# Hybrid decoder trunk: shared expert's up tiles rounded and subtracted behind the normalized chunks, and another order of eviction and subtraction in the second layer's mixer norm

## The chip, the cores and the metric

One Trainium2 chip, one core of it. The metric is the device time of one execution in microseconds (us), less is better. The program is a single launch that reads all inputs from HBM and writes the final output. The names used for the engines are TensorE (PE in the rows, PEld for its weight loads), VectorE (DVE), ScalarE (ACT), GpSimd (POOL) and SyncE (SP), whose queue issues most DMAs.

## What is computed

Two layers over a sequence of 256 tokens with 1024 features, all in float32. Each layer is a token mixer and a mixture of experts (MoE); before each stands an RMSNorm with a scale and a shift per feature. The first layer's mixer is differential attention, the second's is retention.

```python
for i in range(DEPTH):                       # DEPTH = 2
    mod = jax.nn.silu(c) @ ada_w[i] + ada_b[i]
    sh_a, sc_a, g_a, sh_f, sc_f, g_f = jnp.split(mod[:, None, :], 6, axis=-1)
    h = rmsnorm(x, norm_mix[i]) * (1.0 + sc_a) + sh_a
    y = diff_attention(h, ...) if i == 0 else retention(h, ...)
    x = x + g_a * y
    h = rmsnorm(x, norm_ffn[i]) * (1.0 + sc_f) + sh_f
    x = x + g_f * moe(h, ...)
return rmsnorm(x, final_norm)

def moe(xm, router_w, router_b, w1, w3, w2, s_w1, s_w3, s_w2):
    scores = jax.nn.sigmoid((xt @ router_w).astype(jnp.float32))
    choice = scores + router_b        # the best 4 of 8 groups, then the best 8 of 64 experts
    ...
    shared = (jax.nn.silu(xt @ s_w1) * (xt @ s_w3)) @ s_w2
    return (acc[:T] + shared).reshape(B, S, D)
```

The routed experts' part, `acc`, gathers each expert's tokens, runs its two up products and its down product, and adds the weighted result. The shared expert runs over all tokens; its up weights `s_w1` and `s_w3` are 1024x256 each, and the change is about them.

## The kernel before

**Products in three parts.** The products of the mixers, the router and the shared expert's up layer are done with both operands split in two: a rounded high part and the rest. `product` (line 936) issues three matmuls for each: high times high, high times low, low times high. So a weight tile of 128x2048 is handled twice before TensorE may use it: ScalarE rounds it (`round_w`, line 634, the cast on line 637, semaphore `w_hi`), and VectorE subtracts the rounded copy from the tile and leaves the low part in its place (`low_part`, lines 1407 to 1410, semaphore `w_lo`). The tiles have one fixed order, `split` (line 315), which is the order in which both semaphores count.

**The norm.** There are four norms ahead of the last one; their number n is 0 for the first layer's mixer, 1 for its MoE, 2 for the second layer's mixer, 3 for its MoE. For each of the two blocks of 128 tokens ScalarE squares and takes a root (`norm_stats`, line 587), VectorE takes the reciprocal and scales (`norm_root`, lines 1397 and 1402), TensorE turns the block with eight 128x128 transposes (`turn_h`, line 920). The turned input is eight chunks of 128 features in four PSUM banks, two chunks (a pair, m = 0 to 3) in a bank. Then in `evict_hT` ScalarE evicts pairs 0 and 2 with scale and shift (line 612), VectorE pairs 1 and 3 (line 1419), each two instructions of 128x256. ScalarE rounds each pair (line 622, `hT_rounded`; it waits for pairs 1 and 3 on VectorE's `hT_dve`), and VectorE's `low(m)` subtracts (line 1426, `hT_split`). TensorE's next products take the pairs in order and wait in `hT_there` (line 932) for each pair's `low`.

**The MoE's head.** After norm 1 or 3 TensorE computes the router's logits, 24 matmuls (line 938 by way of `product`, from line 1003). ScalarE takes the sigmoid (line 687), TensorE turns the scores back (line 1011), and VectorE does the routing in a long chain of small instructions that begins with the copy on line 1471 and has the chosen experts ready at line 1501. TensorE meanwhile computes the first half of the shared up product, tile 0, 48 matmuls; it waits for that tile's `w_lo`. Then it waits for the chosen experts (`chosen_ready`), ranks them with a few small matmuls (lines 1018 to 1025), does half of tile 1's product (24 matmuls), places the experts (lines 1031 and 1032), and does the other half. VectorE then writes the table of experts and passes (line 1538, `route_ready`). ScalarE's Silu of the up product (line 691) gives two ring slots free (`release(2)`), for which SP has DMAs of expert weights waiting; further expert loads wait for `route_ready`. After the shared down product (line 1045) the loop over experts begins.

**Order.** All orders around the change are written out by hand: each engine's queue is in program order, and semaphores join them. On ScalarE `moe(l)` (line 671) issued the rounding of tile 0 ahead of `norm_stats`, the rounding of tile 1 right behind it, then the table load for Sigmoid with a dummy instruction (line 677), then `evict_hT`. On VectorE `moe(l)` (line 1452) issued `norm_root`, tile 0's `low_part`, `evict_hT`, tile 1's `low_part`; in the first layer a small addition (`later_rows(9)`, line 1620) follows, and then the routing. In norms with n > 0 VectorE's `evict_hT` issued `evict(1)`, `low(0)` only after it, `evict(3)`, then `low(1)` to `low(3)`. `part_high` (line 683) makes bf16 copies for the routed experts and isn't needed until line 1460.

Of the kernel before, what the change touches and what calls it, by code (L numbers as in the profile page):

```python
# [59 lines left out]
def trunk(nc, x, c, norm_mix, norm_ffn, ada_w, ada_b, da_w_in, da_w_out, da_lq1, da_lk1, da_lq2, da_lk2,  # L60
# [18 lines left out]
    with ExitStack() as ctx:  # L79
# [492 lines left out]
        def _(act):  # L572
# [61 lines left out]
            def round_w(*key):  # L634
                if key in split:
                    arrived(act, where[key])
                    nc.scalar.copy(high_of(key), slot(where[key])).then_inc(w_hi, 1)
# [33 lines left out]
            def moe(l):  # L671
# [1 line left out]
                    load_root_table()  # L673
                round_w("shared", l, 0)
                norm_stats()
                round_w("shared", l, 1)
                nc.scalar.activation(lexp[:, 0:1], ident[:, 0:1], ACT.Sigmoid)
                if l == 0:
                    release_ada(9)
                evict_hT()  # L680

                def part_high(tc):
                    nc.scalar.copy(parts[:, tc, 0, :], h[:, tc, :]).then_inc(part_hi, 1)

                part_high(0)
                act.wait_ge(logits_done, l + 1)
                nc.scalar.activation(scoreT, banks[0][:, 0:T], ACT.Sigmoid).then_inc(scoresT_ready, 1)
                part_high(1)
                nc.scalar.activation(lexp[:, 0:1], ident[:, 0:1], ACT.Silu)
                act.wait_ge(sh_up, l + 1)  # L690
# [81 lines left out]
            for part in range(3):  # L772
                n, i = 4 * part, 3 * part + 2
# [605 lines left out]
        def _(dve):  # L1379
# [32 lines left out]
            def evict_hT():  # L1412
                n = norms[0] - 1

                def evict(m):
                    dve.wait_ge(h_turned, 4 * n + m + 1)
                    for kk in range(2):
                        k = 2 * m + kk
                        ins = nc.vector.tensor_scalar(hT_full[:, k, :], banks[m][:, T * kk:T * kk + T],
                                                      mod_T[:, n // 2, 3 * (n % 2) + 1, k:k + 1],  # L1420
                                                      mod_T[:, n // 2, 3 * (n % 2), k:k + 1], ALU.mult, ALU.add)
                    ins.then_inc(hT_dve, 1)
# [4 lines left out]
                                            hT_hi[:, 2 * m:2 * m + 2, :], ALU.subtract).then_inc(hT_split, 1)  # L1427

                dve.wait_ge(mod_T_in[n], 1 if n == 0 else 16)
                evict(1)  # L1430
                if n == 0:
                    low_part("mix_in", 0, 0)
                low(0)
                if n > 0:
                    evict(3)
                for m in range(1, 4):
# [14 lines left out]

            def moe(l):
                norm_root()
                low_part("shared", l, 0)
                evict_hT()
                low_part("shared", l, 1)

                def rest_part(tc):
# [380 lines left out]
```

## Time and profile before

| | us |
|---|---|
| median of 3 runs | 1429.36 (1429.16 to 1429.58) |
| time of the profiled execution | 1428.65 |
| its span in the profile | 1426.9 |
| TensorE matmul busy | 1328.6 (93% of the span) |
| VectorE busy | 550.8 (39%) |
| ScalarE busy | 448.5 (31%) |
| HBM read | 514.10 MB, 361 GB/s over the span |

Stages of the profiled execution, from the page's 40 slices and the timeline: the first layer's mixer up to 198 us, its MoE head from 198 to 236, its loop over experts to 698, the second layer's mixer with its norm to 913.5, its MoE head to about 950, its experts and the last norm to the end. In the expert loops the DMA engines are busy all the time (422 GB/s in the slices); in the second mixer they have room (119 GB/s in the lowest slice), and TensorE is busy in all slices.

How to read it: the share of an engine over the whole span says little, since the stages have different limits. In a head or a norm the engines hand work to one another, and what counts is which of two queues comes last to a meeting point. A time in a timeline row is where the first instruction of the row starts, the next number how long the row takes; a number in brackets is the idle time before it with what ended that idle time.

### The profile page before, as it was taken

The page shows a single profiled execution, that of the slowest core. Times are in us where ns is not written, and L with a number is a line of the kernel's source. Part 1 is how long each engine was busy: PE and PEld are TensorE (multiplying, and loading weights), DVE is VectorE, ACT ScalarE, POOL GpSimd, SP SyncE. Part 2 cuts the span into 40 slices and gives each one's busy share as a digit, 9 for nine tenths or more (in the row PEclk, how much of TensorE's full clock was granted, in tenths as well). Part 3 has the DMA queues.
Part 4 walks back from the last instruction along what each step waited for, and adds up shares of the span by engine and source line. Part 5 has one row for each costly group of instructions (what it writes and reads, how often), then busy time and mean ns, then how long its engine had stood idle before and what let it go on. Part 6 is the DMA issues. An engine that isn't in the chain of part 4 may idle for free.

```text
span 1426.9 us, 32982 instructions
## 1 busy us (share of the span) xinstructions
PE 1328.6 (93%) x12029; PEld 875.0 (61%) x12030; DVE 550.8 (39%) x1227; ACT 448.5 (31%) x890; POOL 207.6 (15%) x663
## 2 busy tenths in 40 slices
PE   4999889999999999989799999799999999999996
PEld 2877666555556555544599998665555555555553
DVE  2556565332323322222534455653332323322334
ACT  3443451222222222221444454522222222222222
POOL 8200102111111111111000000011111111111110
PEclk8999999999999999999899999899999999999999
DMA  9999995999999999999995434449999999999995
GB/s 351 352 385 398 407 383 224 421 421 422 422 422 422 422 422 422 422 422 421 376 298 188 159 119 148 162 181 421 420 422 422 422 421 422 422 422 422 422 422 216
DMA packets 113338, 516.06 MB, mean 362 GB/s; under 512 B 9632, under 2 KB 46624, under 8 KB 63360
## 3 DMA queue, kind: packets, MB, share of 16 engines
q1 hardware_dynamic: 109920, 509.64, 89.1%
q0 software_dynamic: 2656, 3.49, 0.9%
q10 hardware_dynamic: 704, 2.10, 0.4%
q8 instruction: 44, 0.72, 0.2%
q14 instruction: 14, 0.11, 0.0%
HBM read 514.10 MB, written 1.09 MB: 361 GB/s over the span
## 4 chain that ended last, share of the span: by engine, by line
PE 68%; DMA 11%; SPq 6%; DVE 5%; ACT 5%; issue 3%; POOL 1%; ACTq 1%; DVEq 0%; POOLq 0%
PE bank L938 18%; PE bank L1120 15%; PE bank L1141 7%; PE bank L1123 7%; PE bank L1055 6%; DMA ring<-in_exp_w_dram 6%; PE bank L1096 5%; PE bank L1147 3%; SPq L347 3%; DMA ring<-in_da_w_in_dram 2%; DMA mods<-in_exp_w_dram 2%; SPq L350 2%; PE bank L913 2%; DVE arena L1579 1%; PE bank L1130 1%
## 5 line engine op out<-in xcount | busy, mean ns | idle before, releaser
L1120 PE MATMUL bank<-ring,arena 128*64 128x512 f32 x768 | 178.6, 605 | 9.9 <-DMA ring<-in_exp_w_dram 9.9
L1096 PEld LDWEIGHTS bank<-arena 128*128 128x128 bf16 x3264 | 142.1, 98 | 55.5 <-issue 55.0
L1055 PE MATMUL bank<-arena_r 128*128 128x512 f32 x560 | 161.2, 418 | 3.0 <-DVE arena_r L1591 3.0
L1591 DVE TENSOR_TENSOR arena_r<-bank,arena_r 128x512 fp32r<-128x512 f32 x136 | 94.0, 692 | 154.2 <-ACT arena_r L726 154.2
L1096 PE MATMUL bank<-arena 128*128 128x64 bf16 (+1 forms) x3264 | 151.8, 207 | 0.0
L719 ACT ACTIVATE arena<-bank 128x256 f32<-128x256 f32 (+1 forms) x68 | 22.6, 333 | 387.4 <-PE bank L1120 270.1
L726 ACT CAST arena_r<-bank 128x512 fp32r<-128x512 f32 x136 | 79.7, 586 | 189.4 <-PE bank L1141 124.8
L543 POOL TENSOR_TENSOR arena<-arena,pass_base 128x2 f32 x136 | 23.6, 197 | 743.2 <-PE bank L1107 729.2
L1055 PEld LDWEIGHTS bank<-arena_r 128*128 128x128 f32 x560 | 94.6, 188 | 60.2 <-issue 47.5
L938 PE MATMUL bank<-HH_r,ring_r 128*128 128x256 f32 x448 | 128.4, 287 | 0.0
L1120 PEld LDWEIGHTS bank<-ring,arena 128*64 128x64 f32 x768 | 56.5, 139 | 111.4 <-issue 110.8
L1565 DVE TENSOR_SCALAR arena<-bank,mod_T 128x128 f32<-128x128 f32 x272 | 92.9, 404 | 72.0 <-PE bank L1096 72.0
L714 ACT ACTIVATE arena<-bank,mod_T 128x128 f32<-128x128 f32 x272 | 102.5, 457 | 53.2 <-PE bank L1096 53.2
L1579 DVE SCALAR_TENSOR_TENSOR arena<-bank,arena 128x256 f32<-128x256 f32 x35 | 23.5, 671 | 236.8 <-ACT arena L719 236.8
L1123 PE MATMUL bank<-ring,arena 128*32 128x256 f32 x1472 | 91.5, 390 | 7.8 <-ACT arena L714 7.8
L938 PE MATMUL bank<-HH_r,mods_r 128*128 128x256 f32 x288 | 84.5, 293 | 6.2 <-DVE mods_r L1426 6.2
L938 PEld LDWEIGHTS bank<-HH_r,ring_r 128*128 128x128 f32 x448 | 88.0, 196 | 0.0
L1141 PE MATMUL bank<-ring,arena 128*64 128x512 f32 x384 | 87.7, 598 | 0.0
L1123 PEld LDWEIGHTS bank<-ring,arena 128*32 128x32 f32 x1472 | 76.0, 108 | 13.8 <-issue 8.8
L938 PE MATMUL bank<-mods_r 128*128 128x256 f32 x288 | 83.3, 289 | 0.0
L1120 PE MATMUL bank<-mods,arena 128*64 128x512 f32 x176 | 77.8, 595 | 3.8 <-DMA mods<-in_exp_w_dram 3.8
L938 PE MATMUL bank<-HH_r 128*128 128x256 f32 x272 | 78.6, 289 | 0.3 <-DVE ring_r L1409 0.3
(273 smaller groups left out, 2158.3 us busy)
## 6 DMA issues: line engine op xcount, KB each, us to landing
ring<-in_exp_w_dram SPq DMA_DIRECT2D x264, 1024.0 KB, 24.0
ring<-in_ada_w_dram SPq DMA_DIRECT2D x48, 1024.0 KB, 13.6
HH<-in_exp_w_dram SPq DMA_DIRECT2D x40, 1024.0 KB, 21.0
mods<-in_exp_w_dram SPq DMA_DIRECT2D x40, 1024.0 KB, 25.0
arena<-in_exp_w_dram SPq DMA_DIRECT2D x40, 1024.0 KB, 25.1
ring<-in_ret_w_in_dram SPq DMA_DIRECT2D x24, 1024.0 KB, 11.9
ring<-in_da_w_in_dram SPq DMA_DIRECT2D x12, 1024.0 KB, 17.3
ring<-in_ret_w_out_dram SPq DMA_DIRECT2D x8, 1024.0 KB, 4.9
```

Source lines behind the costliest of these rows:

```text
L347: sp.dma_start(place.rearrange("p (k n) -> p k n", k=KD), w.rearrange("o (p k) n -> p (o k) n", k=KD)).then_inc(done, 16)
L714: ins = nc.scalar.activation(to, got, ACT.Identity, scale=mod_T[:, l, 4, k:k + 1], bias=mod_T[:, l, 3, k:k + 1])
L726: nc.scalar.copy(y[:, 0, 512 * hf:512 * hf + 512], banks[hf][:, :]).then_inc(u["y_hi"], 1)
L938: ins = nc.tensor.matmul(out, a[x1], b[x2], start=(first and i == 0), stop=(last and i == 2), skip_group_check=True)
L1055: ins = nc.tensor.matmul(banks[4 + NH * tc + hf][:, :], S[:, P * tc:P * tc + P], y[:, r, 512 * hf:512 * hf + 512], start=False, stop=(last ...
L1096: ins = nc.tensor.matmul(banks[2 - 2 * half][:, P * kk:P * kk + 2 * W], parts[:, tc, r, P * (4 * half + kk):P * (4 * half + kk + 1)], Pg[: ...
L1120: ins = nc.tensor.matmul(banks[1][W * i:W * i + W, :], xg[:, k, W * i:W * i + W], w13[j][:, k, :, :], start=(k == 0), stop=(k == KD - 1))
L1123: ins = nc.tensor.matmul(banks[1][W * i:W * i + W, 0:256], xg[:, k, W * i:W * i + W], w13[j].rearrange("p k w (n b) -> p k b w n", b=2)[:, ...
L1141: ins = nc.tensor.matmul(banks[hf][W * j:W * j + W, :], ehT[:, b, W * j:W * j + W], w2[j][:, b, 512 * hf:512 * hf + 512], start=(b == 0), ...
L1147: ins = nc.tensor.matmul(banks[hf][W * i:W * i + W, :], ehT[:, 0, W * i:W * i + W], w2[j][:, b, 512 * hf:512 * hf + 512], start=True, stop ...
L1565: ins = nc.vector.tensor_scalar(to, got, mod_T[:, l, 4, k:k + 1], mod_T[:, l, 3, k:k + 1], ALU.mult, ALU.add)
L1591: nc.vector.tensor_tensor(y[:, 1, 512 * hf:512 * hf + 512], banks[hf][:, :], y[:, 0, 512 * hf:512 * hf + 512], ALU.subtract).then_inc(u[f" ...
```

## The change

Three edits, in two functions on ScalarE and VectorE:

1. ScalarE, both MoE heads: the rounding of the shared expert's second up tile moves behind `evict_hT`, and `part_high(0)` behind the sigmoid of the logits.
2. VectorE, both MoE heads: the subtraction of the shared expert's first up tile moves behind `evict_hT`, so that both tiles' subtractions stand there, one behind the other.
3. VectorE, norm 2 only (the second layer's mixer): `low(0)` is issued ahead of `evict(1)`.

No instruction is added or removed, and no semaphore's count changes. TensorE's, GpSimd's and SP's instructions are the same as before.

```diff
@@ ScalarE, moe(l)
                 round_w("shared", l, 0)
                 norm_stats()
-                round_w("shared", l, 1)
                 nc.scalar.activation(lexp[:, 0:1], ident[:, 0:1], ACT.Sigmoid)
                 if l == 0:
                     release_ada(9)
                 evict_hT()
+                round_w("shared", l, 1)
 
                 def part_high(tc):
                     nc.scalar.copy(parts[:, tc, 0, :], h[:, tc, :]).then_inc(part_hi, 1)
 
-                part_high(0)
                 act.wait_ge(logits_done, l + 1)
                 nc.scalar.activation(scoreT, banks[0][:, 0:T], ACT.Sigmoid).then_inc(scoresT_ready, 1)
+                part_high(0)
                 part_high(1)
@@ VectorE, evict_hT()
                 dve.wait_ge(mod_T_in[n], 1 if n == 0 else 16)
-                evict(1)
+                if n != 2:
+                    evict(1)
                 if n == 0:
                     low_part("mix_in", 0, 0)
                 low(0)
+                if n == 2:
+                    evict(1)
                 if n > 0:
                     evict(3)
                 for m in range(1, 4):
@@ VectorE, moe(l)
                 norm_root()
+                evict_hT()
                 low_part("shared", l, 0)
-                evict_hT()
                 low_part("shared", l, 1)
```

**The change on VectorE in the first layer's MoE head**, from the reciprocal of the second token block to the start of the routing. `ring2` is the ring slot with the shared expert's first two tiles, `arena_r` their rounded copies, `mods`, `HH_r` and `mods_r` the normalized chunks, their high and their low part. Before:

```order
L1397 RECIPROCAL rs<-rs 128x1 [waits root]
L1402 TENSOR_SCALAR HH<-X,rs 128x1024 [waits dve_step]
L1409 TENSOR_TENSOR ring2_r<-ring2,arena_r 128x2048 [waits w_hi]
L1419 TENSOR_SCALAR mods<-bank1,mod_T 128x256 [waits h_turned,mod_T_in1]
L1419 TENSOR_SCALAR mods<-bank1,mod_T 128x256
L1426 TENSOR_TENSOR mods_r<-mods,HH_r 128x512 [waits hT_rounded]
L1419 TENSOR_SCALAR mods<-bank3,mod_T 128x256 [waits h_turned]
L1419 TENSOR_SCALAR mods<-bank3,mod_T 128x256
L1426 TENSOR_TENSOR mods_r<-mods,HH_r 128x512 [waits hT_rounded] x3
L1409 TENSOR_TENSOR ring2_r<-ring2,arena_r 128x2048 [waits w_hi]
L1620 TENSOR_TENSOR mods<-bank4,mods 128x256 [waits ada_done]
L1471 COPY arena<-bank2 128x128 [waits bank_rows_read,late_consts_in,scores_ready]
```

Now:

```order
L1397 RECIPROCAL rs<-rs 128x1 [waits root]
L1402 TENSOR_SCALAR HH<-X,rs 128x1024 [waits dve_step]
L1419 TENSOR_SCALAR mods<-bank1,mod_T 128x256 [waits h_turned,mod_T_in1]
L1419 TENSOR_SCALAR mods<-bank1,mod_T 128x256
L1426 TENSOR_TENSOR mods_r<-mods,HH_r 128x512 [waits hT_rounded]
L1419 TENSOR_SCALAR mods<-bank3,mod_T 128x256 [waits h_turned]
L1419 TENSOR_SCALAR mods<-bank3,mod_T 128x256
L1426 TENSOR_TENSOR mods_r<-mods,HH_r 128x512 [waits hT_rounded] x3
L1409 TENSOR_TENSOR ring2_r<-ring2,arena_r 128x2048 [waits w_hi] x2
L1623 TENSOR_TENSOR mods<-bank4,mods 128x256 [waits ada_done]
L1474 COPY arena<-bank2 128x128 [waits bank_rows_read,late_consts_in,scores_ready]
```

The first 128x2048 subtraction has moved from ahead of the chunks to behind them; both now stand between the last chunk's `low` and the routing. Lines from 1430 on are three higher in the changed kernel.

**The change on ScalarE in the same place**, from the last root of the norm to the sigmoid of the logits. Before:

```order
L601 ACTIVATE rs<-ss,eps 128x1 [waits sumsq]
L637 CAST arena_r<-ring2 128x2048 [waits landed5]
L677 ACT_TABLE_LOAD
L677 ACTIVATE lexp<-ident 128x1
L612 ACTIVATE mods<-bank0,mod_T 128x256 [waits ada_done,h_turned,mod_T_in1]
...
L622 CAST HH_r<-mods 128x512 [waits hT_dve]
L683 CAST arena<-HH 128x1024
L687 ACTIVATE arena<-bank0 128x256 [waits logits_done]
L683 CAST arena<-HH 128x1024
```

Now:

```order
L601 ACTIVATE rs<-ss,eps 128x1 [waits sumsq]
L676 ACT_TABLE_LOAD
L676 ACTIVATE lexp<-ident 128x1
L612 ACTIVATE mods<-bank0,mod_T 128x256 [waits ada_done,h_turned,mod_T_in1]
...
L622 CAST HH_r<-mods 128x512 [waits hT_dve]
L637 CAST arena_r<-ring2 128x2048 [waits landed5]
L686 ACTIVATE arena<-bank0 128x256 [waits logits_done]
L683 CAST arena<-HH 128x1024 x2
```

The cast of the 128x2048 tile has moved from ahead of the table load to behind the last chunk's cast, and the first bf16 copy behind the sigmoid.

## Rows read from the trace of the kernel before

**Rows 1.** The profile's page, the chain that ended last, share by engine.

```profile
PE 68%; DMA 11%; SPq 6%; DVE 5%; ACT 5%; issue 3%; POOL 1%; ACTq 1%; DVEq 0%; POOLq 0%
```

**Rows 2.** Timeline of VectorE, first MoE head: start, us, line, shapes, [idle before <- releaser].

```profile
204.43 2.28 DVE L1409 TENSOR_TENSOR ring_r<-ring,arena_r 128x2048 fp32r<-128x2048 f32 x1
...
208.01 0.69 DVE L1426 TENSOR_TENSOR mods_r<-mods,HH_r 128x512 fp32r<-128x512 f32 x1 [0.39 <-ACT HH_r L622]
...
211.33 2.28 DVE L1409 TENSOR_TENSOR ring_r<-ring,arena_r 128x2048 fp32r<-128x2048 f32 x1
213.53 0.42 DVE L1620 TENSOR_TENSOR mods<-bank,mods 128x256 f32<-128x256 f32 x1
214.54 0.29 DVE L1471 COPY arena<-bank 128x128 f32<-128x128 f32 x1 [0.59 <-PE bank L1011]
```

**Rows 3.** Timeline of ScalarE, the same place.

```profile
203.01 1.90 ACT L637 CAST arena_r<-ring 128x2048 fp32r<-128x2048 f32 x1
...
206.32 1.00 ACT L612 ACTIVATE mods<-bank,mod_T 128x256 f32<-128x256 f32 x2
207.36 0.62 ACT L622 CAST HH_r<-mods 128x512 fp32r<-128x512 f32 x1
...
213.62 0.38 ACT L687 ACTIVATE arena<-bank 128x256 f32<-128x256 f32 x1 [2.23 <-PE bank L938]
```

**Rows 4.** Timeline of TensorE, the same place.

```profile
204.57 1.09 PE L925 MATMUL bank<-ident,HH 128*128 128x128 f32 x8 [0.31 <-DVE HH L1402]
208.85 0.46 PE L938 MATMUL bank<-HH_r,arena_r 128*128 128x256 f32 x1 [3.19 <-DVE mods_r L1426]
...
220.36 0.19 PE L1018 MATMUL bank<-arena,upper 128*128 128x64 bf16 x1
```

**Rows 5.** Timeline of VectorE, second MoE head.

```profile
920.96 2.28 DVE L1409 TENSOR_TENSOR ring_r<-ring,arena_r 128x2048 fp32r<-128x2048 f32 x1
...
924.52 0.69 DVE L1426 TENSOR_TENSOR mods_r<-mods,HH_r 128x512 fp32r<-128x512 f32 x1 [0.38 <-ACT HH_r L622]
...
931.18 0.29 DVE L1471 COPY arena<-bank 128x128 f32<-128x128 f32 x1 [1.06 <-PE bank L1011]
```

**Rows 6.** Timeline of TensorE, second MoE head.

```profile
919.69 3.68 PE L925 MATMUL bank<-ident,HH 128*128 128x128 f32 x16 [6.20 <-DVE HH L1402]
925.36 0.55 PE L938 MATMUL bank<-HH_r,arena_r 128*128 128x256 f32 x1 [1.99 <-DVE mods_r L1426]
```

**Rows 7.** Timeline of VectorE, norm 2, the second layer's mixer.

```profile
708.30 0.99 DVE L1419 TENSOR_SCALAR mods<-bank,mod_T 128x256 f32<-128x256 f32 x2
709.21 0.68 DVE L1426 TENSOR_TENSOR mods_r<-mods,HH_r 128x512 fp32r<-128x512 f32 x1
...
710.71 1.88 DVE L1426 TENSOR_TENSOR mods_r<-mods,HH_r 128x512 fp32r<-128x512 f32 x3
```

**Rows 8.** Timeline of ScalarE, norm 2.

```profile
708.14 0.62 ACT L622 CAST HH_r<-mods 128x512 fp32r<-128x512 f32 x1
```

**Rows 9.** Timeline of TensorE, norm 2: the first product's first matmuls.

```profile
710.03 0.55 PE L938 MATMUL bank<-HH_r,mods_r 128*128 128x256 f32 x1 [1.76 <-DVE mods_r L1426]
...
711.45 0.57 PE L938 MATMUL bank<-HH_r,mods_r 128*128 128x256 f32 x1
```

**Rows 10.** Windows: stretch, length, busy us of PE, PEld, DVE, ACT, POOL, PEclk, DMA share, GB/s.

```profile
172.50:178.20 5.70, 5.70 (x14) 4.44 (x15) 2.89 (x7) 3.47 (x6) 2.75 (x4) 0.50 1.03 407
208.85:212.36 3.51, 3.51 (x16) 3.33 (x17) 3.51 (x6) 2.54 (x5) 0.00 (x0) 0.51 1.02 429
212.36:213.60 1.24, 1.23 (x10) 1.02 (x9) 1.24 (x2) 0.00 (x0) 0.00 (x0) 1.00 1.00 423
371.30:377.40 6.10, 3.42 (x17) 1.44 (x18) 0.53 (x3) 0.00 (x0) 1.58 (x4) 1.00 1.01 419
550.40:557.00 6.60, 3.96 (x13) 1.58 (x14) 0.49 (x3) 0.00 (x0) 1.58 (x4) 0.75 1.01 422
710.00:714.10 4.10, 4.07 (x18) 4.01 (x19) 3.42 (x6) 3.12 (x4) 0.00 (x0) 0.50 1.09 349
```

## The prediction

> **What bounds the kernel now.** I read the page first, for the chain that ended last: TensorE holds 68% of it, and VectorE and ScalarE 5% each [rows 1]. Those small shares are the norms and the MoE heads, where the change lies. There the chain goes from queue to queue, so I read the timelines of three engines at three places, and ask at each what comes last.
>
> *First MoE head.* ScalarE casts the second up tile (203.01, 1.90 us) before it may load its table and evict the first pair at 206.32 [rows 3]. VectorE spends 2.28 us on the first tile from 204.43 on [rows 2]. But the eight transposes of the second block are through at 204.57 + 1.09 = 205.66 [rows 4], so both engines are late for the chunks. The first product starts at 208.85 after 3.19 us of standstill [rows 4], the sigmoid follows at 213.62 [rows 3], and the routing at 214.54, where VectorE has idled for 0.59 us [rows 2]. Until then the meeting point is TensorE's and ScalarE's. From 214.54 on it is VectorE's: the ranks' matmul at 220.36 [rows 4] waits for the routing, and the rest of the head for the ranks. So the question is not when the first product starts, but **when VectorE can start the routing**.
>
> *Second MoE head.* The same: first product at 925.36 [rows 6], routing at 931.18 after 1.06 us idle [rows 5].
>
> *Norm 2.* Here TensorE goes from the first product at 710.03 [rows 9] straight into the mixer, so a later stream of products is a later end.
>
> **First MoE head, worked out.** Edits 1 and 2 go together. ScalarE reaches its table load at 203.01 instead of 204.91; load and dummy take what they took from there to 206.32, 1.41 us, so it is free at 204.42. The transposes are spaced (1.09 - 0.28)/7 = 0.12 us, taking 0.28 for one; the second of the block ends at about 205.0, and the first eviction starts there instead of at 206.32. From that start to `low(0)` it took 208.01 - 206.32 = 1.69 us (the cast at 207.36 with 0.62 lies between) [rows 2, 3], so `low(0)` runs at 206.72, 1.29 us earlier, with VectorE's `evict(1)` (from 205.25, some 0.99 long) done in time. The first product moves with it, to 207.56.
>
> Now VectorE's account. From `low(0)` to the end of the last `low` are 211.33 - 208.01 = 3.32 us, so 210.04. Then come **two** tile subtractions instead of one, each 213.53 - 211.33 = 2.20 us: 214.44. `later_rows` takes 0.42, and the routing starts at about 214.90 instead of 214.54 [rows 2]. **Term: +0.36 us.** The work is the same; the idle time has moved from behind it (0.59) and `low(0)` (0.39) to ahead of the evictions, where it can't be used, and there is slightly more of it. TensorE isn't last any more: even with all 24 logits matmuls at the low clock its logits end by about 212.4, 1.2 us before 213.62, and the scores are there 0.92 us later (213.62 to 214.54), at 213.3. `part_high(0)` costs nothing: it moves into ScalarE's wait behind the sigmoid. Tile 0's low part is ready at 212.3 instead of 206.7, and TensorE, behind the scores' transposes, wants it between 212 and 213, so this hardly costs; tile 1's cast on ScalarE now ends at about 211.0, ahead of VectorE's need at 212.24.
>
> **Second MoE head.** The transposes run slower here, 16 in 3.68 us [rows 6], spaced 0.21 us, so the tenth, which ends the first pair, is there at 922.1. `low(0)` is at 922.14 + 1.69 = 923.83, only 0.69 us earlier than 924.52. Then 3.32 and twice 2.20: 931.55, and with nothing between, the routing starts at 931.57 instead of 931.18 [rows 5]. **Term: +0.39 us.**
>
> **Norm 2 (edit 3).** VectorE is free at 708.30 [rows 7]. The cast it needs ends at 708.14 + 0.62 = 708.76 [rows 8], so `low(0)` starts at 708.80 instead of 709.21, and the first product at 709.62 instead of 710.03 [rows 9]. But `low(1)` now has two evictions between: 708.80 + 0.60 + twice 0.91 (708.30 to 709.21) = 711.23 instead of 710.71 [rows 7], **0.52 us later**. ScalarE's cast of pair 1 waits for `evict(1)` (done at 710.4) and ends at 711.06, just in time. TensorE does its first six matmuls from 709.62, stands still from about 711.0, and starts the second pair at 711.45 + 0.52 = 711.97 or a little later [rows 9]. All later products are behind that.
>
> What this costs depends on the clock. TensorE is at 0.50 here until 714.1, so at 1.2 GHz, then at 2.4 [rows 10]. A matmul takes 3.51/16 = 0.22 us at the lower and 1.24/10 = 0.12 at the higher level [rows 10], so a microsecond at the lower loses 0.45 us. If the clock rises at 714.1 as before, the lag of 0.52 shrinks to about 0.52 x 0.12/0.22 = 0.29 us. But the rise came 4.1 us after the products began (710.03 to 714.1), elsewhere 3.5 us (208.85 to 212.36) and 5.7 us (172.50 to 178.20) [rows 10], each after an unbroken run of matmuls. The run is broken now. If it has to begin anew at 712.0, the rise is at 715.5 to 717.7 instead of 714.1: 1.4 to 3.6 us more at the lower level, a loss of 0.6 to 1.6, middle 1.1. I take that, since every row with a rise has an unbroken run before it. **Term: 0.29 + 1.1 = +1.4 us**, bounds +0.2 (rise unchanged, a little of the first product's gain kept) and +1.9.
>
> **Sum.** 0.36 + 1.4 + 0.39 = +2.15 us. None of it is absorbed behind: the expert loads that SP holds back come after Silu and after `route_ready`, so they move along with the head, and TensorE and the DMA queues alternate on the chain from there on. The profiled execution (1428.65 us) would become 1430.8; the median of the runs before is 0.71 us above it, and I forecast against the median: **1431.5 us**, +0.15%. A measurement of this kernel can tell about 0.2%, 2.9 us, from no change.
>
> **Rivals.**
>
> *The clock falls in the new hole: slower.* TensorE did tile 0's 48 matmuls right up to the ranks at 220.36; now it is done with them 1.2 to 1.9 us sooner and waits for a routing that starts 0.36 later. That makes a standstill of about 1.8 to 2.2 us in the first head and 1.0 to 1.5 in the second. The rows show both outcomes of somewhat longer ones: after 2.7 us at 371.30 the clock stayed at 1.00, after 2.6 us at 550.40 it fell (0.75 over the stretch of 6.6, so about 3.3 us at the lower level) [rows 10]. If it falls here, 3.4 us at 1.2 GHz lie on tile 1's 48 matmuls, which release ranks, Silu and the expert loads: 3.4 x 0.45 = 1.5 us each time. It decides from one such fall on top of my sum: 2.15 + 1.5 = 3.65, 1433.0 us; with both 1434.5. For it: a hole only 0.5 us shorter than one that fell. Against: of two such holes only one fell, and these are shorter. Chance 0.22.
> The Trainium skill ("TensorE: Matmul & The Clock Gate", "Why this matters for your kernels") advises to avoid long idle gaps between bursts of matmuls, with a bound longer than any hole named here; by it no fall would come and 1431.5 would stand, yet the hole at 550.40 is under its bound and fell, so the row decides and the rival keeps its chance.
>
> *The clock rises at 714.1 as before in norm 2.* The sum is 0.36 + 0.29 + 0.39 = 1.04: 1430.4 us. For it: the second run is interrupted for only a microsecond. Chance 0.22.
>
> *TensorE, not VectorE, was what the routing waited for, and stays it: faster.* Then the earlier first products count in full: -1.29 and -0.69, with +0.29 in norm 2: -1.7, 1427.7 us. The idle 0.59 and 1.06 us before the routing speak for it; against it that 2.20 us of tile work now stand where only that idle time was. It would need VectorE's two subtractions to cost 1.1 us each. Chance 0.04.
>
> *The shift of the heads is absorbed* in the expert loops, whose DMA runs all the time, and the norm's by nothing: about 1429.4 to 1430.8. Chance 0.07. That the change doesn't do what it says is excluded by the orders shown.
>
> **How the numbers follow.** The forecast case (1431.5, bounds 1430.3 to 1432.3 from norm 2's term and a few tenths on the others) has 0.45. The range takes in the two mild cases below it and the fall with one loss above it: 1429.4 to 1433.5, which leaves out the faster case, the double fall and about half a tenth more at each end. Faster by over 0.2% (under 1426.5) is reached by no case but luck with the clock: 0.03. Slower by over 0.2% (over 1432.2) holds the clock's fall, 0.22, and the top of the forecast case, 0.04: 0.26. Within 0.2%: 0.71.
>
> **What would show it.** In both heads: `low(0)` about 1.3 and 0.7 us earlier against the transposes; VectorE without idle time before line 1474; line 1018 some 0.4 us later; TensorE idle before it for 1 to 2.2 us, with PEclk telling about the rival. In norm 2: a hole of about 1 us behind the first six matmuls, and PEclk at 0.50 beyond 714.5. I am wrong if the routing starts earlier than before against the transposes' end, if the hole behind the six matmuls isn't there, or if the expert loops take a different time.

## The result, and the profile after

The changed kernel took 1432.42 us (median of 8 runs, 1430.72 to 1434.42), the kernel before beside it 1429.08 (8 runs, 1428.36 to 1429.58): a ratio of 1.0024, 95% interval 1.0013 to 1.0035. The change costs 3.3 us by the medians; the interval alone would allow 1.9 to 5.0. Its profiled execution took 1432.12 us, 3.5 more than that of before.

I cut both profiles into stages. Each head is measured from the start of line 1402 on the second token block, the last thing ahead of the transposes on VectorE. "Routing" is the start of the copy with which VectorE's routing chain begins (line 1471, now 1474), "shared down" the first matmul of the shared down product (line 1045), and a hole is a stretch in which TensorE stands still:

| us | before | after | difference |
|---|---|---|---|
| span start to head 1's scaling | 203.33 | 204.44 | +1.11 |
| head 1: scaling to `low(0)` / first product / routing | 4.68 / 5.52 / 11.21 | 3.46 / 4.30 / 11.81 | -1.22 / -1.22 / +0.60 |
| head 1: scaling to first matmul of shared down | 25.32 | 25.92 | +0.60 |
| from there to norm 2's scaling (experts, same code) | 476.37 | 476.28 | -0.09 |
| norm 2: scaling to `low(0)` / first product | 4.19 / 5.01 | 3.84 / 4.68 | -0.35 / -0.33 |
| norm 2 and mixer ("mixer stage" below), to head 2's scaling | 214.84 | 216.41 | +1.57 |
| head 2: scaling to `low(0)` / first product / routing | 4.66 / 5.50 / 11.32 | 4.04 / 4.88 / 11.77 | -0.62 / -0.62 / +0.45 |
| head 2: scaling to first matmul of shared down | 25.44 | 25.87 | +0.43 |
| rest (same code) | 481.63 | 481.47 | -0.16 |

In all three places the first product is earlier, and what counts behind it is later. The +1.11 at the start is in code that the change doesn't touch. There the profiles scatter from 202.4 to 204.6 in all kernels but the two that put work on GpSimd.

VectorE's timeline of the changed kernel, first head (start, us, line, shapes, [idle before <- releaser]), for [rows 2]:

```profile
206.42 0.99 DVE L1419 TENSOR_SCALAR mods<-bank,mod_T 128x256 f32<-128x256 f32 x2 [0.82 <-PE bank L925]
207.90 0.69 DVE L1426 TENSOR_TENSOR mods_r<-mods,HH_r 128x512 fp32r<-128x512 f32 x1 [0.48 <-ACT HH_r L622]
...
211.22 4.49 DVE L1409 TENSOR_TENSOR ring_r<-ring,arena_r 128x2048 fp32r<-128x2048 f32 x2
215.62 0.42 DVE L1623 TENSOR_TENSOR mods<-bank,mods 128x256 f32<-128x256 f32 x1
216.25 0.29 DVE L1474 COPY arena<-bank 128x128 f32<-128x128 f32 x1 [0.21 <-DVE mods L1623]
```

The 0.59 us ahead of the routing are gone, and 0.82 stand ahead of the evictions in their place. What is left ahead of line 1474 is released by VectorE itself. The chain that ended last, same place (start, us, engine, what, line), now runs through VectorE from `low(0)` to the routing; its pieces from `low(1)` to line 1623:

```profile
209.50 1.80 DVE mods_r L1426 x3
211.30 4.40 DVE ring_r L1409 x2
215.71 0.35 DVE mods L1623
```

TensorE's timeline there, for [rows 4], and two windows (stretch, length, busy us of PE, PEld, DVE, ACT, POOL, PEclk, DMA share, GB/s):

```profile
208.74 0.36 PE L938 MATMUL bank<-HH_r,arena_r 128*128 128x256 f32 x1 [1.99 <-DVE mods_r L1426]
...
222.07 0.19 PE L1018 MATMUL bank<-arena,upper 128*128 128x64 bf16 x1 [1.42 <-DVE arena L1504]
```

```profile
220.60:222.10 1.50, 0.09 (x3) 0.07 (x3) 1.22 (x8) 0.00 (x0) 0.10 (x1) 1.00 0.66 251
222.10:225.00 2.90, 2.90 (x28) 2.83 (x29) 2.26 (x15) 0.00 (x0) 0.77 (x2) 1.00 0.16 59
```

The hole ahead of the ranks is there, 1.42 us, and in this execution the clock stayed up behind it. Norm 2, for [rows 7, 9, 10]: VectorE, TensorE, a window.

```profile
710.48 0.69 DVE L1426 TENSOR_TENSOR mods_r<-mods,HH_r 128x512 fp32r<-128x512 f32 x1 [0.48 <-ACT HH_r L622]
711.09 1.90 DVE L1419 TENSOR_SCALAR mods<-bank,mod_T 128x256 f32<-128x256 f32 x4
712.90 1.89 DVE L1426 TENSOR_TENSOR mods_r<-mods,HH_r 128x512 fp32r<-128x512 f32 x3
```

```profile
711.32 0.55 PE L938 MATMUL bank<-HH_r,mods_r 128*128 128x256 f32 x1 [1.43 <-DVE mods_r L1426]
...
713.64 0.58 PE L938 MATMUL bank<-HH_r,mods_r 128*128 128x256 f32 x1 [0.70 <-DVE mods_r L1426]
```

```profile
711.30:718.50 7.20, 6.48 (x29) 6.21 (x29) 5.78 (x8) 3.46 (x5) 0.00 (x0) 0.50 1.09 351
```

The four evictions now stand between `low(0)` and `low(1)`, TensorE stands still for 0.70 us behind its first six matmuls, and the clock stays at 0.50 for 7.2 us after the start of the first product instead of 4.1. The second pair's products start 7.00 us after the scaling instead of 6.43.

### The profile page after: what moved, and what is told of

Same layout as the page of the kernel before. It is cut to its first block, busy times and chain, and to the rows that moved or that the text cites. A ratio compares the mean times of both kernels' runs of the same rounds, so it can differ in the third digit from the quotient of the medians.

```text
span 1430.4 us, 32982 instructions
## 1 busy us (share of the span) xinstructions
PE 1330.2 (93%) x12029; PEld 877.2 (61%) x12030; DVE 550.8 (39%) x1227; ACT 448.8 (31%) x890; POOL 208.0 (15%) x663
## 4 chain that ended last, share of the span: by engine, by line
PE 70%; DMA 11%; DVE 7%; ACT 4%; SPq 4%; issue 3%; ACTq 1%; DVEq 0%
PE bank L938 18%; PE bank L1120 16%; PE bank L1141 8%; PE bank L1123 7%; PE bank L1055 6%; DMA ring<-in_exp_w_dram 6%; PE bank L1096 5%; PE bank L1147 4%; SPq L347 2%; DMA mods<-in_exp_w_dram 2%; PE bank L913 2%; DVE arena L1582 1%; DMA ring<-in_ada_w_dram 1%; DVE ring_r L1409 1%; DMA ring<-in_da_w_in_dram 1%
```

## The experiments

My theory: VectorE's queue sets the routing in the heads (edit 2 costs, edit 1 gives), and the broken stream in norm 2 delays the clock. The rivals: TensorE or the clock sets the routing; the clock falls in the new hole. Edit 1 is ScalarE's reordering, edit 2 VectorE's in `moe`, edit 3 that in norm 2. Every kernel computes all of the reference. A run's own milestones count from the same line 1402 as in the table. Each ratio comes with its 95% interval and is not the quotient of the two medians beside it; where the two differ, the ratio counts.

**Edit 1 alone.**

```
-                round_w("shared", l, 1)
                 nc.scalar.activation(lexp[:, 0:1], ident[:, 0:1], ACT.Sigmoid)
                 evict_hT()
+                round_w("shared", l, 1)
...
-                part_high(0)
                 act.wait_ge(logits_done, l + 1)
                 nc.scalar.activation(scoreT, ...)
+                part_high(0)
```

> ScalarE's edit alone (edit 1), VectorE as before. My theory, that VectorE's queue decides in the changed heads: here only one tile subtraction stands ahead of the routing's copy behind the chunks, so VectorE has room; low(0) starts where VectorE's tile subtraction and its first eviction are done, 0.47 us earlier in the first head and 0.45 in the second, and TensorE stays what the routing waits for: routing 0.4 to 0.5 us earlier in both heads, 0.9 us less in all, about 1428.2 against 1429.1. Rival, that the later rounding of tile 1 on ScalarE is itself what delays the routing or tile 1's product: no gain or up to 0.5 us more per head, 1429 to 1430.

Measured: 1427.96 us (11 runs) beside 1428.73 for before (35 runs); ratio 1.0000 (0.9991 to 1.0008). First products 0.51 and 0.48 us earlier, the routing only 0.11 and 0.24. The gain expected of edit 1 is mostly not there. Where it went, the kernel with edit 1 and fills tells, further down.

**Edit 2 alone.**

```
                 norm_root()
+                evict_hT()
                 low_part("shared", l, 0)
-                evict_hT()
                 low_part("shared", l, 1)
```

> VectorE's head edit alone (edit 2), ScalarE as before. My theory: ScalarE still evicts as late as before, so low(0) doesn't move, and VectorE has two tile subtractions (2 x 2.20 us) behind the chunks: routing at 211.33 + 4.40 + 0.42 + 0.2 for the completion of later_rows = 216.35 against 214.54 in the first head (+1.8), and 927.84 + 4.40 = 932.25 against 931.18 in the second (+1.1): +2.9 us, about 1432. Rival, that TensorE's first product decides: no change, since the first product starts as before, 1429.1.

Measured: 1433.21 us (12 runs), ratio 1.0027 (1.0015 to 1.0039). The routing is 1.82 us later in head 1 and 1.07 in head 2. The first products did not move (5.52 and 5.50 us). Its holes ahead of line 1018 are 1.92 and 0.68 us. Behind the first the clock fell: from routing to shared down 15.58 us instead of 14.11. VectorE and TensorE, first head:

```profile
212.60 4.49 DVE L1409 TENSOR_TENSOR ring_r<-ring,arena_r 128x2048 fp32r<-128x2048 f32 x2
...
217.63 0.29 DVE L1471 COPY arena<-bank 128x128 f32<-128x128 f32 x1 [0.21 <-DVE mods L1620]
...
223.43 0.19 PE L1018 MATMUL bank<-arena,upper 128*128 128x64 bf16 x1 [1.92 <-DVE arena L1501]
```

**Edits 1 and 2**, norm 2 as before.

> Edits 1 and 2 together, norm 2 as before. My theory: the heads of the changed kernel as profiled, routing +0.60 us in the first and +0.4 in the second against the norm's end: +1.0 us, about 1430.1, with the rest of the changed kernel's +3.3 in norm 2. Rival, that the clock's fall in TensorE's new hole ahead of the ranks makes most of the loss: +2.5 to +4 us here, and PEclk under 1.00 over tile 1's product in the profile.

Measured: 1430.38 us (11 runs), ratio 1.0011 (1.0002 to 1.0021). The routing stands at 11.81 and 11.77 us, as in the changed kernel to 0.01. In head 1 the clock fell. TensorE's timeline and windows of this kernel:

```profile
221.19 0.19 PE L1018 MATMUL bank<-arena,upper 128*128 128x64 bf16 x1 [1.55 <-DVE arena L1501]
```

```profile
219.30:221.20 1.90, 0.35 (x4) 0.18 (x4) 1.61 (x9) 0.00 (x0) 0.18 (x2) 1.00 0.51 172
221.20:222.40 1.20, 1.20 (x13) 1.14 (x14) 0.67 (x5) 0.00 (x0) 0.80 (x2) 1.00 0.42 167
222.40:225.80 3.40, 3.40 (x18) 3.40 (x17) 2.08 (x13) 0.00 (x0) 0.00 (x0) 0.50 0.02 6
225.80:229.00 3.20, 3.20 (x28) 3.01 (x27) 2.38 (x7) 0.00 (x0) 0.00 (x0) 1.00 0.00 0
```

After a hole of 1.55 us the granted clock went to 0.50 for 3.4 us, in the middle of tile 1's products. Shared down came at 27.39 instead of 25.92: 1.47 us, where the rival said 1.5. The Trainium skill ("TensorE: Matmul & The Clock Gate", "Why this matters for your kernels") warns of gaps longer than this one; here the row decides, and a shorter gap was enough.

**Edit 3 alone.**

```
-                evict(1)
+                if n != 2:
+                    evict(1)
...
                 low(0)
+                if n == 2:
+                    evict(1)
```

> Edit 3 alone: low(0) ahead of evict(1) in norm 2. My theory: low(1) is 0.5 to 0.6 us later, TensorE stands still for about 0.7 us behind its first six matmuls, and the clock rises later: between +0.3 (rise unmoved) and +1.9 us, middle +1.4 to +1.6, about 1430.6, and with more spread from run to run than before, since the moment of the rise decides. Rival, that norm 2 costs only the 0.5 us of the later pair: +0.3 to +0.5 us and no more spread, 1429.5.

Measured: 1429.83 us (12 runs), ratio 1.0006 (0.9998 to 1.0015). Mixer stage 216.09 us, 1.25 more than before; median 1.1 more, 0.9 by the ratio, with zero just inside the interval.

**Tile 0's subtraction on GpSimd.** The changed kernel, with VectorE doing tile 1 alone.

```
+            def pool_low_part(*key):
+                pool.wait_ge(w_hi, split.index(key) + 1)
+                pool.wait_ge(w_lo, split.index(key))
+                nc.gpsimd.tensor_tensor(slot_r(where[key]), slot(where[key]), high_of(key), ALU.subtract).then_inc(w_lo, 1)
...
                 evict_hT()
-                low_part("shared", l, 0)
+                dve.wait_ge(w_lo, split.index(("shared", l, 1)))
                 low_part("shared", l, 1)
```

> The changed kernel with one of the two tile subtractions taken off VectorE: GpSimd does tile 0 (it stands idle there), VectorE tile 1. My theory, that VectorE's queue decides when the routing starts in the changed heads: one 2.20 us less on it, so the routing starts when the scores are there, 1.0 to 1.3 us sooner in each head than in the changed kernel (10.5 to 10.8 us after the second block's scaling instead of 11.8), TensorE's hole ahead of the ranks shrinks to under 0.5 us, and the whole is 2 to 3 us under the changed kernel, about 1429 to 1429.5 with norm 2 as changed. Rival, that the scores decide: routing within 0.2 us of 11.8, no gain. What could spoil the test: VectorE's instructions longer while GpSimd works.

Measured: 1435.63 us (6 runs) beside 1429.25 for before (21 runs), ratio 1.0039 (1.0025 to 1.0054). The test was spoiled by what it put in. GpSimd's subtraction, and VectorE's scaling beside it and without it:

```profile
199.91 4.85 POOL L520 TENSOR_TENSOR ring_r<-ring,arena_r 128x2048 fp32r<-128x2048 f32 x1 [22.41 <-ACT arena_r L646]
```

```profile
201.42 4.27 DVE L1411 TENSOR_SCALAR HH<-X,rs 128x1024 f32<-128x1024 f32 x1
...
205.80 1.16 DVE L1411 TENSOR_SCALAR HH<-X,rs 128x1024 f32<-128x1024 f32 x1
...
214.29 2.29 DVE L1418 TENSOR_TENSOR ring_r<-ring,arena_r 128x2048 fp32r<-128x2048 f32 x1 [0.94 <-ACT arena_r L646]
```

VectorE's scaling took 4.27 us instead of 1.16, and the stages that hold the two stalls are longer by some 2 us each (205.80 us to head 1's scaling, mixer stage 218.25). Counted from the second block's scaling, which comes behind the stall, the heads can still be read: the routing stood at 11.33 and 11.26 us, 0.5 before the changed kernel's, the holes ahead of the ranks were 0.85 and 0.11 us, and the clock fell behind neither. That is against the rival (within 0.2 of 11.8), and less than the 1.0 to 1.3 us expected: with one subtraction VectorE waited 0.94 us for ScalarE's cast of tile 1.

**TensorE kept busy, in the kernel before and in the changed one.** Matmuls of a constant against itself ahead of and behind the transposes, into a bank that is unused there:

```
+            def fill(count, bank):
+                for _ in range(count):
+                    nc.tensor.matmul(bank[:, 0:P], ident[:, :], ident[:, :], start=True, stop=True)
             def turn_h():
+                fill({2: 36, 3: 44}.get(norms[0], 0), banks[3])
...
+                fill({1: 14, 2: 20, 3: 14}.get(norms[0], 0), banks[5])
```

> The kernel before with idle stretches of TensorE filled: matmuls of identity by identity into a bank that nobody reads then, 36 and 44 ahead of the transposes of norms 2 and 3, and 14, 20, 14 behind those of norms 1, 2, 3. It computes the same. My theory, that the lower clock is what makes norm 2 and part of the heads long: PEclk 1.00 through norm 2, 16 transposes of norm 3 in about 2.2 us instead of 3.68, the mixer stage shorter by 1.5 to 2.2 us, the heads' routing 0.5 to 1.5 us earlier, 3 to 4.5 us less in all, about 1425, and less spread between runs. Rival, that the filling only delays the transposes or leaves the clock as it is: the same or slower, 1428.7 to 1431.

> The changed kernel with the same filling. My theory: with the clock held up, edit 3 costs nothing any more (ScalarE's cast of pair 0 is there when VectorE is free, low(1) within 0.1 us of the filled kernel before, and TensorE catches up at 2.4 GHz): mixer stage within 0.3 us of the filled kernel before, instead of +1.6 us unfilled. The heads still wait for VectorE's two tile subtractions, and worse against the filled kernel before, where the routing is no longer held by low-clock products: +1 to +2 us over both heads. Rival, that edit 3's cost is the later pair itself and not the clock: +0.5 us or more in the mixer stage here too.

Measured: 1431.27 us (12 runs), ratio 1.0010 (1.0001 to 1.0020), and 1434.10 (10 runs), ratio 1.0032 (1.0023 to 1.0041). The fills were too long. TensorE in norm 2, with the fill of before:

```profile
697.91 8.20 PE L922 MATMUL bank<-ident 128*128 128x128 f32 x72
```

36 matmuls show as 72 passes of 0.11 us. In norm 2 the first product came 8.07 us after the scaling instead of 5.0, in head 2 at 8.1 instead of 5.5. Only head 1 can be read. In the kernel before, the first product is unmoved at 5.52 and the routing at 10.83 instead of 11.21. The higher clock on the logits brings 0.38 us, and then VectorE's own queue is the limit, with nothing but the 0.21 us of waiting for its own last subtraction ahead of the routing. In the changed kernel the fill put off the first product from 4.30 to 5.20, and the routing stayed at 11.82: TensorE's start doesn't set it there.

**Both subtractions on GpSimd**, edit 1, norm 2 as before.

> Edit 1 (ScalarE), norm 2 as before, and both tile subtractions of each head on GpSimd, none on VectorE. My theory: routing when the scores are there, 0.5 to 1 us earlier than in the kernel before in both heads, 1 to 2 us less in all, about 1427.5; TensorE's tile 0 product then waits for GpSimd only if its subtraction takes over 8 us. Rival: GpSimd's subtraction is so slow (over 4 us) that tile 1 comes after the ranks and TensorE waits for it, or it slows VectorE beside it: no gain or slower.

Measured: 1437.22 us (6 runs), ratio 1.0056 (1.0037 to 1.0076). Low parts come so late that shared down stands at 28.18 and 29.19 us, and in norm 2's stage and at the start VectorE is held again. It can't tell where the routing would be, but the clock fell behind both of its holes ahead of the ranks, 1.56 and 2.91 us.

**Fills of the right length** (20 and 22 ahead of norm 2's and head 2's transposes, 10, 11 and 10 behind those of head 1, norm 2, head 2): in the kernel before, with edit 1 alone, and in the changed kernel. They are called held, since with the fills the granted clock is 1.00 from the transposes to the routing in both heads, and all through the mixer stage.

> The kernel before with a filling cut to size: each fp32 matmul of identity by identity shows as two passes of 0.11 us, so 20 and 22 ahead of the transposes of norms 2 and 3, and 10, 11, 10 behind those of norms 1, 2, 3. My theory: nothing is delayed (first products 5.5, 5.0, 5.5 us after the second block's scaling, as in the kernel before), PEclk 1.00 through both heads and norm 2; the first head's routing is then VectorE's account alone, 4.68 + 3.32 + 2.20 + 0.63 = 10.83 us, the second head's 4.66 + 3.32 + 2.24 = 10.2 instead of 11.3, and the mixer stage 1.3 us shorter than 214.84: 2.8 us less in all, about 1426.3. Rival, that the clock's level in these places isn't worth it, because the chain lies on VectorE and ScalarE there: 0 to 1 us less.

> Edit 1 alone with the same filling. My theory: edit 1's earlier chunks weren't worth more because TensorE ran the logits at the lower clock; with the clock held, the routing follows VectorE's account: 4.18 + 3.32 + 2.20 + 0.63 = 10.3 us in the first head, 9.7 to 9.8 in the second: 0.4 to 0.5 us per head under the held kernel before, about 1425.3, under both kernels. Rival: the later cast of tile 1 on ScalarE delays VectorE's second subtraction (VectorE idle ahead of it), no gain over the held kernel before.

> The changed kernel with the same filling. My theory: edit 3's cost is the clock's, so the mixer stage is within 0.3 us of the held kernel before; the heads' routing stays on VectorE's account with two subtractions behind the chunks: 11.8 us in the first head (1.0 over the held kernel before) and 11.1 in the second (+0.9), and TensorE's hole ahead of the ranks is longer, 2 us and more, so that the clock may fall there for another 1.5 us: 2 to 4 us over the held kernel before, 1428.2 to 1430. Rival, that edit 3 costs by the later pair itself: mixer stage +0.5 us or more.

Measured, beside 1428.74 for before (29 runs):

| | us | ratio (interval) | first product, heads | routing, heads | mixer stage |
|---|---|---|---|---|---|
| before, held | 1426.24 (12 runs) | 0.9979 (0.9971 to 0.9988) | 5.52, 5.52 | 10.84, 10.29 | 213.69 |
| edit 1, held | 1427.07 (11) | 0.9984 (0.9975 to 0.9993) | 5.02, 5.02 | 11.11, 10.49 | 213.69 |
| changed, held | 1430.85 (12) | 1.0011 (1.0002 to 1.0021) | 4.30, 4.30 | 11.82, 11.19 | 213.95 |

Here the clock on the logits can't be the reason any more. First products 0.50 and 1.22 us earlier go with routings 0.2 to 0.3 and 0.9 to 1.0 us **later**. For edit 1, VectorE's timeline of that kernel tells why:

```profile
208.18 1.89 DVE L1432 TENSOR_TENSOR mods_r<-mods,HH_r 128x512 fp32r<-128x512 f32 x3
...
210.75 2.29 DVE L1415 TENSOR_TENSOR ring_r<-ring,arena_r 128x2048 fp32r<-128x2048 f32 x1 [0.69 <-ACT arena_r L637]
```

VectorE waits 0.69 us for ScalarE's cast of tile 1, which edit 1 has put behind the chunks. So edit 1's gain at the front is given back at the next meeting of the two engines. TensorE in the held changed kernel, first head and norm 2:

```profile
220.64 0.19 PE L1024 MATMUL bank<-arena,upper 128*128 128x64 bf16 x1 [2.48 <-DVE arena L1510]
```

```profile
713.05 0.38 PE L944 MATMUL bank<-HH_r,mods_r 128*128 128x256 f32 x1 [1.21 <-DVE mods_r L1432]
```

In norm 2 the changed kernel's hole grew to 1.21 us (0.47 in the held kernel before), and still it cost only 213.95 - 213.69 = 0.26 us. That is how much later the second pair's products start (6.68 us after the scaling instead of 6.42): with the clock at the higher level from the start, nothing of edit 3 but this lag is left. Behind the holes of the heads, 2.48 and 1.83 us, the clock fell both times (routing to shared down 15.60 and 15.58 us).

**The hole ahead of the ranks filled**, and nothing else, in the changed kernel:

```
                     if i == 1:
+                        fill(4, banks[5])
                         pe.wait_ge(chosen_ready, l + 1)
```

> The changed kernel with only its new hole filled: four matmuls of identity by identity (0.9 us) ahead of TensorE's wait for the chosen experts in both heads, everything else as changed, norm 2 unfilled. It computes the same. My theory, that the hole lets the clock fall in about half of the heads (5 of 10 in the profiles of kernels with edit 2, none of 12 without it) at 1.48 us each: no fall in either head here, 14.1 us from the routing's copy to the down product in both, the routing itself where it was (11.8 us), and the median 1 to 2 us under the changed kernel, about 1430 to 1431 where the kernel before has 1428.7. Rival, that the fall isn't the hole's doing or isn't on the path: median as the changed kernel's (+3.3), or a fall seen in a head in spite of the filling.

Measured: 1431.16 us (11 runs) beside 1428.26 for before (15 runs), ratio 1.0014 (1.0005 to 1.0023). TensorE's timeline, first head:

```profile
219.16 1.05 PE L922 MATMUL bank<-ident 128*128 128x128 f32 x8
...
220.66 0.20 PE L1023 MATMUL bank<-arena,upper 128*128 128x64 bf16 x1 [0.44 <-DVE arena L1509]
```

The routing stays at 11.82 and 11.77 us, the hole shrinks to 0.44, and the clock fell in neither head (14.03 and 14.02 us from routing to shared down). The point estimate drops from 1.0024 to 1.0014, about 1.4 us, but the intervals overlap, they come from different experiments, and over the kernel before beside each the medians differ by only 0.4 us (+3.3 and +2.9). In the profile the cure did what was expected, though the changed kernel's own profile had no fall either; the times only point the same way.

## Why the prediction was right, and where it wasn't

**The number.** Forecast 1431.5 us, range 1429.4 to 1433.5; measured 1432.42, inside the range. As a difference it is less good: +2.15 us forecast, +3.3 measured. The direction and the two places of the loss were forecast for the reasons that the runs show; a third component, the falling clock, stood only as a rival, and the range holds the result with its help.

**The bound in the heads: right.** "When can VectorE start the routing" was the right question, and with both subtractions behind the chunks VectorE's own queue is the answer. Edit 2 alone made the routing later by 1.82 and 1.07 us with no change on ScalarE; the first products of the changed kernel were 1.22 and 0.62 us earlier (predicted 1.29 and 0.69) and the routing still later. The rival by which TensorE goes on setting the routing is dead: in the filled kernel the first product was put off by 0.9 us, and the routing didn't move. (The sum by which that rival needed subtractions of 1.1 us was off: 213.25 - 0.42 - 210.04, halved, is 1.4. With 2.20 measured it changes nothing.) Another reading was wrong too. The logits were to end by 212.4 even with all 24 matmuls at the low clock; 207.56 + 24 x 0.22 is 212.8, and measured from the scaling they ended 9.53 us behind it instead of 10.26, only 0.7 us sooner, not 1.2. That costs the routing nothing, but it makes the hole shorter: tile 0's products ended 0.72 and 0.44 us sooner, not 1.2 to 1.9, and the holes were 1.42 and 0.96 us where 1.8 to 2.2 and 1.0 to 1.5 were forecast.

**Head 1's term, +0.36: undersized.** It measured +0.60. The sum left out the 0.21 us for which VectorE stands idle until the completion of its own line 1623 (after, `[0.21 <-DVE mods L1623]`). Before, that wait was hidden in the 0.59 us of waiting for the scores [rows 2]. I counted the removed idle time, not a second wait under it. **Head 2's term, +0.39,** measured +0.45 at the routing and +0.43 at shared down.

**Norm 2's term, 0.29 + 1.1.** The lag was right in kind: the second pair's products started 0.57 us later, forecast 0.52. That the stage cost 0.26 with the clock held is close to 0.29 by luck, for there the lag itself was 0.26 and not 0.52. For the clock, 7.2 us to the rise instead of 4.1 is inside the 1.4 to 3.6 us more that I named, and the stage measured +1.57 against +1.4. How much of it belongs to the change is less sure. In the four profiles whose norm 2 is that of before, without fills and without work on GpSimd, the clock was up for good 4.1 to 6.0 us after the first product's start, and the stage scattered from 214.84 to 215.71; in edit 3's three profiles without fills in norm 2 it was so after 6.5, 7.2 and 7.2 us, and the stage took 216.09, 216.41 and 216.41, more than in any of the four. Edit 3 alone gives 0.9 us by the ratio. So 0.9 to 1.6 us, most of it clock; seven profiles can't say more.

**The step that fell short: a forecast case without a fall.** I gave the fall of the clock in the new hole a chance of 0.22 as an alternative. It comes in about half of the heads instead, and belongs into the sum as a share. Profiles with edit 2 and no fill in the hole show ten heads. The clock stayed up behind holes of 0.68, 0.72, 0.96, 1.42 and once 1.83 us, and fell behind 1.55, 1.83, 1.92 and twice 2.48 us. It also fell in the two heads with both subtractions on GpSimd, behind 1.56 and 2.91. In 12 heads with VectorE's old order (before, edit 1, edit 3 and the fills in them) it never fell, and their longest hole was 1.40 us. So it is the length of the hole that goes with the fall; the order of the work only makes the hole. Each fall costs 1.48 us; the rival's 3.4 x 0.45 = 1.5 was right to a few hundredths. The changed kernel's own profile happened to have none. Its runs spread over 3.7 us, those of before beside them over 1.2 (in the other experiments before spread by up to 6.6, so the spread alone proves nothing).

The account: 1.03 in the heads, 0.9 to 1.6 in norm 2, together 1.9 to 2.6; measured 3.3, with an interval (1.9 to 5.0) that would bear the sum without any fall. The rest, 0.7 to 1.4 us, would be 0.5 to 0.9 falls in an execution. Other kernels point the same way. Edits 1 and 2 cost 1.6 us by the ratio, 1.03 of it at the routing; edit 2 alone 3.9, 2.9 of it at the routing: 0.4 and 0.7 falls are left. In the held pair the mean granted clock over all executions was 0.9887 before (12 runs) and 0.9868 changed (12 runs). A fall of 3.4 us lowers the mean of an execution by 0.5 x 3.4/1429 = 0.0012, so the difference would be, as an estimate, 1.6 falls, give or take 0.8; the mean times differ by 4.4 us, and 2.1 of lag leave 1.5 falls. For the profiled execution the sum is another one: 1.03 + 1.57 + 1.11 at the start of the program - 0.09 - 0.16 = 3.5, and the 1.11 is chance. How often the clock falls in an execution of the changed kernel as it is stays open.

**Absorbed behind: no.** The same code behind the heads took 0.09 and 0.16 us less. Behind first heads that were later still (shared down at 27.4 us) the expert loop took 475.94 to 476.36 us, as in the kernel before (476.37), so the lag passes through in full.

**Edit 1** gives nothing that the times can show: ratio 1.0000, where I had counted on some 0.9 us when I ran it, and 0.35 us at the two routings of its profile. In head 1 VectorE meets the moved cast 0.69 us too early; in head 2 the routing still waits 0.49 us for the scores, whose matmuls, started 0.48 us earlier, ran at a lower mean clock (0.64 instead of 0.67 from the first product to the routing) and ended only 0.24 us earlier.

## What to carry to other kernels

Work that an engine does ahead of a meeting with another engine, in time in which it would idle, costs nothing; moved behind the meeting it adds to the queue for which the next one waits. Before moving it back, add up the engine's whole queue to its next meeting, completion waits included. An earlier start of TensorE can be worth less than nothing if the burst is then broken: count the holes that the move leaves, and put the cost of a fall (1.48 us here) into the sum with its chance. The better change to this kernel left all orders alone: filling TensorE's idle time around the transposes with harmless matmuls gave 2.5 us by the medians (ratio 0.9979), faster than both kernels here.

## What the runs showed of the hardware that I had not expected

**GpSimd held VectorE until it was done.** A 128x2048 subtraction on GpSimd takes 4.85 us, VectorE 2.29 for the same. VectorE's 128x1024 scaling that started beside it took 4.27 us instead of 1.16 and ended at 205.69, 0.93 after GpSimd's end at 204.76, almost as if it had begun only then. It was so in all four places where the two met (3.92 us in the second heads). The Trainium skill ("SBUF — State Buffer", "Who interferes with whom") calls the port pair that the two share an exclusive lock, whose loser blocks fully, and counts VectorE's `tensor_scalar` among the instructions that can take it, in some of its modes. The trace agrees with the full block; which mode the scaling ran in, no run shows.

**Holes of 1.55 us are enough for a fall, and not every one of 1.83 makes one.** Of the eight holes ahead of the ranks of 1.55 us or more, seven were followed by a fall; of those up to 1.42 us none was. A fall lasted 3.4 us.

**Transposes alone raised the clock, and it didn't stay.** Windows of norm 2 with edit 1 alone:

```profile
699.50:702.90 3.40, 0.00 (x0) 0.00 (x0) 3.33 (x6) 2.15 (x4) 0.45 (x1) 1.00 1.10 348
702.90:706.30 3.40, 2.83 (x14) 2.77 (x15) 3.08 (x4) 1.06 (x4) 0.63 (x1) 0.50 1.10 348
706.30:709.70 3.40, 1.29 (x10) 1.02 (x9) 3.40 (x7) 3.26 (x8) 0.00 (x0) 1.00 1.07 371
709.70:713.10 3.40, 2.93 (x15) 2.78 (x14) 2.72 (x4) 2.42 (x2) 0.00 (x0) 0.50 1.10 348
```

The granted clock was at the higher level while TensorE idled, fell, rose behind nothing but transposes (from 703.47 on), and fell again under the products that had begun at 708.9. So the level at which a burst starts isn't told by the burst itself.

**The same first stage, from 202.4 to 204.6 us.** Code that no edit touches scatters by 2 us from profile to profile, as much as most effects here. The first expert loop lies at 475.9 to 476.4 us in ten of the profiles and at 477.8 to 478.0 in four (edit 2 alone, edit 3 alone, tile 0 on GpSimd, edit 1 with fills); why, stays open. Only milestones counted from a point close by could tell the edits apart.
